# Gate bound in columns, an early convolution tile, decays two units ahead, and forget-gate sums moved forward

## The chip, the cores and the metric

The kernel runs on one core of a Trainium2 chip. The metric is device time in microseconds, the median of several runs. The five engines are TensorE (PE), VectorE (DVE), ScalarE (ACT), GpSimd (POOL) and SyncE (SP, which here issues the weight transfers). PE's weight loads are a sixth row of the profile, PEld.

## The reference

All of it is fp32, on 256 positions of width 1024. Two blocks follow each other: the first has an HGRN2 mixer, a SwiGLU, a differential attention and a mixture of eight experts; the second has a Conformer convolution, two squared-ReLU networks and a "forgetting" attention. The parts that the change touches, cut:

```python
# HGRN2: 8 heads of 128; lb_logits is (3, 1024)
q, f, i, g = split(h @ w_in, 4)
lb = cumsum(softmax(lb_logits, axis=0), axis=0)[0]
forget = lb + (1 - lb) * sigmoid(f);  log_f = log(forget);  k = 1 - forget
q = silu(q);  v = i
# per head, causal: out[t] = sum over s<=t of (q[t] * exp(sum of log_f over s+1..t)) . k[s]  v[s]
o = rms_norm(o, norm_g) * sigmoid(g);  h @ w_out follows

# Conformer convolution
u = hn @ w_pw1 + b_pw1;  a, g = split(u, 2);  u = a * sigmoid(g)
u = depthwise_causal_conv(u, w_dw, width 31) + b_dw;  layernorm, silu, @ w_pw2

# forgetting attention, 16 heads of 64
logit[t, s] = q_t.k_s / 8 + c[t] - c[s],  c = cumsum(log_sigmoid(h @ w_f + b_f))
```

## The kernel before

The program is one fixed order of instructions per engine, tied by semaphores; nothing reorders it. Its backbone is a product of fp32 matrices in three passes: every weight half of 2048 columns is split by ACT (`wh`, L762) and DVE (`wl`, L1292) into a high and a low part, the input is split in the same way (`xTh`, `xTl`), and PE adds three products (L1920 to L1922). Three `wh`/`wl` slots are used in turn. ACT and DVE each have a function `split()`, and the n-th split of DVE waits for the n-th of ACT. Each call stands by hand between other work. SP refills three weight slots of 2 MB.

A projection is a row of units (one chunk of 512 output columns, two halves of the weights, two blocks `b` of 128 positions). The results go to the two banks of `up`; the first half of the next unit waits until DVE has moved the bank of the same `b` on.

**HGRN2 projection, units 0 to 7** (0 to 126 us). The order of the chunks is `HG_CHUNKS`: 0 and 1 are q, 2 and 3 the forget gate, 4 and 5 v, 6 and 7 the output gate. The lower bound `lb` is worked out beside it: GpSimd broadcasts the three rows of logits to all 128 partitions, and DVE and ACT handle them as 128x1024 tiles (L1366 to L1380, L867). For a gate chunk DVE runs four operations per block (L1345 to L1348), ACT the sigmoid (L801) and the logarithm (L862).

**HGRN2 recurrence** (131 to 227 us). Sixteen steps m = 2*head + block. For each, PE makes the decays ("levels", L2107, four products of 512 columns into the banks `level_banks(n)`), ACT takes the exponential (L883), DVE multiplies it with q and k (L1399 to L1405, the tiles `hgA`, `hgB`), PE makes the scores into `acc[:, 2:4]` (L2123, L2126), DVE masks them into `hgS` (L1414), and PE adds up the output (L2135, L2137, "outs"). The score banks and `hgS` exist once. So the scores of m+1 wait for the mask of m, and the mask of m waits for the scores of m and for the outs of m-1 (semaphores `hg_s`, `hg_o`).

**Convolution** (1777 to 1902 us). A projection of 4 units (L1742, L1073, L1748 per block), and then 31 taps for each of 8 channel tiles. DVE does tiles 0 to 3 with 31 multiply-adds each (`tap`, L1728, L1730), a few of them between its units. PE does tiles 4 to 7 as products with diagonal matrices (L2372), which ACT writes (L1089) into a ring of 16; ACT also adds the bias (L1082). After that PE waits for both (`cv_dw`, `cv_sum`).

**Second attention** (from 2247 us). The running sums `c` of the forget gate come from small products (L2410 to L2416) placed in the q projection's second unit; ACT then copies the key side (L1142) and sends it by two DMAs (L1146) into rows of the key tiles. Queries are copied by L794, the scores are L2427.

Of the kernel before, what the change touches and what calls it, by code (L numbers as in the profile page):

```python
# [32 lines left out]
P = 128  # L33
D = 1024
# [155 lines left out]
def _program(nc, t, ctx):  # L190
# [73 lines left out]
    hg_raw = flat(arena[:, 0:2, :])[:, 0:3 * D].rearrange("p (r n) -> p r n", r=3)  # L264
    lb, omlb = spare[:, 0:D], spare[:, D:2 * D]
# [29 lines left out]
    CV_DVE, CV_PE = range(4), range(4, KT)  # L295
# [17 lines left out]
    hg_cross = tp[:, 0, 0:P]  # L313
# [17 lines left out]
    HG_CHUNKS = [0, 1, 4, 5, 2, 3, 6, 7]  # L331
# [131 lines left out]
    hg_x = sem("hg_x")  # L463
    hg_fh, hg_fl = sem("hg_fh"), sem("hg_fl")
# [28 lines left out]
    def _(sp):  # L493
# [236 lines left out]
    def _(act):  # L730
# [114 lines left out]
        split(SPLITS - 1)  # L845
        for i, c in enumerate(HG_CHUNKS):
            split()
# [15 lines left out]
            split()  # L863
            if i == 1:
                act.wait_ge(s_lbD, 1)
                for r in range(3):
                    ins = f(hg_raw[:, r, :], hg_raw[:, r, :], ACT.Exp)  # L867
                ins.then_inc(s_lbA, 1)
            elif i == 3:
# [6 lines left out]
        for x in range(2 * NB):  # L876
            at = slice((x // NB) * W, (x // NB + 1) * W)
            f(lfh[:, x % NB, at], lf[:, x % NB, at], ACT.Copy).then_inc(hg_fh, 1)
        for n in range(NH * NB + 3):
            if n < NH * NB:  # L880

                act.wait_ge(hg_m, n + 1)
                f(level_banks(n), level_banks(n), ACT.Exp).then_inc(hg_e, 1)  # L883
            if 2 <= n < NH * NB + 2:
                m = n - 2
                j, b = m // NB, m % NB
                act.wait_ge(hg_o, m + 1)
# [1630 lines left out]
```

## Time and profile before

| | |
|---|---|
| median of 3 runs | 2548.72 us (2546.42 to 2553.87) |
| the profiled execution | 2556.3 us, span 2554.5 us, mean granted clock 0.973 |
| busy: PE, PEld | 2392.2 us (94%), 1968.0 us (77%) |
| busy: DVE, ACT, POOL | 1797.1 us (70%), 1465.3 us (57%), 56.7 us (2%) |
| the chain that ended last | PE 75%, DVE 11%, ACT 7%, DMA 5%, issue 2% |

A row of a timeline gives the start in us from the span's start, the time in us that the instructions took, the engine and line, the operation with its output and inputs, how many it merges, and in brackets the idle time before it and who ended that. PE rows overlap: in a full stream one product of 512 columns starts every 0.23 us at the full clock (2.4 GHz) and every 0.43 us at half of it (1.2 GHz). The granted clock is 1.00 or 0.50 at any moment; a number between is a mean.

### The profile page before, as it was taken

The page shows a single profiled execution, that of the slowest core. Times are in us where ns is not written, and L with a number is a line of the kernel's source. Part 1 is how long each engine was busy: PE and PEld are TensorE (multiplying, and loading weights), DVE is VectorE, ACT ScalarE, POOL GpSimd, SP SyncE. Part 2 cuts the span into 40 slices and gives each one's busy share as a digit, 9 for nine tenths or more (in the row PEclk, how much of TensorE's full clock was granted, in tenths as well). Part 3 has the DMA queues.
Part 4 walks back from the last instruction along what each step waited for, and adds up shares of the span by engine and source line. Part 5 has one row for each costly group of instructions (what it writes and reads, how often), then busy time and mean ns, then how long its engine had stood idle before and what let it go on. Part 6 is the DMA issues. An engine that isn't in the chain of part 4 may idle for free.

```text
span 2554.5 us, 29769 instructions
## 1 busy us (share of the span) xinstructions
PE 2392.2 (94%) x11189; PEld 1968.0 (77%) x11189; DVE 1797.1 (70%) x1712; ACT 1465.3 (57%) x1560; POOL 56.7 (2%) x99
## 2 busy tenths in 40 slices
PE   7888999877999999999999999997989998989997
PEld 6677788666788888888888888885777887777886
DVE  5675554674889898989898988887765455554454
ACT  4532444352777777777777777775565446455344
POOL 0000000002300000000000000000010000000000
PEclk9999999998999999999999999998999999999999
DMA  8203554404999999999999999995303544413542
GB/s 296 100 4 116 182 190 167 170 34 151 330 351 370 331 385 325 382 334 378 336 378 336 379 337 369 347 369 192 140 5 132 198 181 165 151 60 132 187 161 80
DMA packets 264116, 589.69 MB, mean 231 GB/s; under 512 B 8417, under 2 KB 39377, under 8 KB 263760
## 3 DMA queue, kind: packets, MB, share of 16 engines
q1 hardware_dynamic: 261376, 579.38, 62.5%
q0 software_dynamic: 2608, 8.93, 1.0%
q8 instruction: 67, 1.10, 0.2%
q14 instruction: 33, 0.27, 0.0%
q10 hardware_dynamic: 32, 0.02, 0.0%
HBM read 587.22 MB, written 1.05 MB: 230 GB/s over the span
## 4 chain that ended last, share of the span: by engine, by line
PE 75%; DVE 11%; ACT 7%; DMA 5%; issue 2%; ACTq 0%; DVEq 0%; SPq 0%
PE up L1920 15%; PE up L1922 14%; PE up L1921 14%; PE acc L1920 7%; PE acc L1922 7%; PE acc L1921 7%; DVE wl L1292 5%; ACT wh L762 4%; DMA raw<-in_ffn_w 4%; PE up L2372 2%; PE acc L2239 1%; PE up L2137 1%; PE acc L2123 1%; PE tp L2275 1%; DVE half L1414 1%
## 5 line engine op out<-in xcount | busy, mean ns | idle before, releaser
L1609 DVE TENSOR_TENSOR wl<-raw,wh 128x2048 fp32r<-128x2048 f32 x378 | 864.7, 2291 | 127.3 <-ACT wh L980 124.6
L980 ACT ACTIVATE wh<-raw 128x2048 fp32r<-128x2048 f32 x378 | 727.1, 1924 | 227.0 <-PE up L1922 137.0
L1920 PE MATMUL up<-wh,xTh 128*128 128x512 f32 x1888 | 761.2, 403 | 46.1 <-DVE wl L1292 8.6
L1922 PE MATMUL up<-wh,xTl 128*128 128x512 f32 x1888 | 745.4, 395 | 0.0
L1921 PE MATMUL up<-wl,xTh 128*128 128x512 f32 x1888 | 744.7, 394 | 0.0
L1292 DVE TENSOR_TENSOR wl<-raw,wh 128x2048 fp32r<-128x2048 f32 x171 | 389.5, 2291 | 388.7 <-ACT wh L762 387.4
L762 ACT ACTIVATE wh<-raw 128x2048 fp32r<-128x2048 f32 x171 | 324.9, 1916 | 383.4 <-PE up L1922 212.2
L1920 PEld LDWEIGHTS up<-wh,xTh 128*128 128x128 f32 x1888 | 361.1, 191 | 129.7 <-issue 35.7
L1922 PEld LDWEIGHTS up<-wh,xTl 128*128 128x128 f32 x1888 | 360.1, 191 | 78.2
L1921 PEld LDWEIGHTS up<-wl,xTh 128*128 128x128 f32 x1888 | 361.4, 191 | 72.2 <-issue 0.7
L1920 PE MATMUL acc<-wh,hTh 128*128 128x512 f32 x848 | 330.2, 389 | 2.3 <-DVE hTl L1629 1.5
L1922 PE MATMUL acc<-wh,hTl 128*128 128x512 f32 x848 | 330.1, 389 | 0.0
L1921 PE MATMUL acc<-wl,hTh 128*128 128x512 f32 x848 | 329.9, 389 | 0.0
L1920 PEld LDWEIGHTS acc<-wh,hTh 128*128 128x128 f32 x848 | 159.2, 188 | 35.6 <-issue 2.7
L1921 PEld LDWEIGHTS acc<-wl,hTh 128*128 128x128 f32 x848 | 159.2, 188 | 33.0
L1922 PEld LDWEIGHTS acc<-wh,hTl 128*128 128x128 f32 x848 | 159.2, 188 | 33.0
L990 ACT ACTIVATE hTh<-tp 128x512 fp32r<-128x512 f32 x63 | 37.8, 600 | 76.6 <-PE tp L2275 76.6
L801 ACT ACTIVATE half<-up,sc 128x512 f32<-128x512 f32 x40 | 27.5, 689 | 55.1 <-PE up L1922 55.0
L2372 PE MATMUL up<-arena 128*128 128x256 f32 x248 | 55.8, 388 | 1.6 <-ACT arena L1089 1.6
L1321 DVE SCALAR_TENSOR_TENSOR xTl<-tp,vecs,xTh 128x128 fp32r<-128x128 f32 x112 | 30.3, 344 | 36.6 <-ACT xTh L782 36.2
L2372 PEld LDWEIGHTS up<-arena 128*128 128x128 f32 x248 | 48.2, 195 | 9.1 <-ACT arena L743 2.0
L1730 DVE SCALAR_TENSOR_TENSOR arena<-arena,wdw 128x256 f32<-128x256 f32 x120 | 51.2, 481 | 1.4
(352 smaller groups left out, 1953.0 us busy)
## 6 DMA issues: line engine op xcount, KB each, us to landing
raw<-in_moe_w_gate SPq DMA_DIRECT2D x126, 1024.0 KB, 6.4
raw<-in_moe_w_up SPq DMA_DIRECT2D x126, 1024.0 KB, 6.9
raw<-in_moe_w_down SPq DMA_DIRECT2D x126, 1024.0 KB, 5.9
raw<-in_ffn_w SPq DMA_DIRECT2D x32, 2048.0 KB, 8.9
raw<-in_hg_w_in SPq DMA_DIRECT2D x7, 2048.0 KB, 13.2
raw<-in_da_w_in SPq DMA_DIRECT2D x6, 2048.0 KB, 8.1
raw<-in_ffn_w_gate SPq DMA_DIRECT2D x11, 1024.0 KB, 6.9
raw<-in_ffn_w_up SPq DMA_DIRECT2D x11, 1024.0 KB, 11.0
```

What stands on the lines that cost most here:

```text
L762: f(wh[:, q % SPLITS, :], raw_half(q), ACT.Copy).then_inc(s_hi, 1)
L801: f(out, in_, func, **kw).then_inc(s_act, 1)
L980: f(wh[:, x % SPLITS, :], raw[:, x % RAW, :], ACT.Copy).then_inc(moe["hi"], 1)
L990: f(hTh[:, 0, :], tp[:, 0, :], ACT.Copy).then_inc(moe["Th"], 1)
L1292: V.tensor_tensor(wl[:, q % SPLITS, :], raw_half(q), wh[:, q % SPLITS, :].bitcast(F32), ALU.subtract).then_inc(s_lo, 1)
L1321: ins = V.scalar_tensor_tensor(lo[:, k, :], x[:, k, :], cols[:, gain, 4 * q + k:4 * q + k + 1], hi[:, k, :].bitcast(F32), ALU.mult, ALU.su ...
L1609: V.tensor_tensor(wl[:, x % SPLITS, :], raw[:, x % RAW, :], wh[:, x % SPLITS, :].bitcast(F32), ALU.subtract).then_inc(moe["lo"], 1)
L1730: ins = V.scalar_tensor_tensor(cT[:, k, :], src, wdw[:, k, j:j + 1], cT[:, k, :], ALU.mult, ALU.add)
L1920: mm(out, x_hi, w_hi, start=start, stop=False)
L1921: mm(out, x_hi, w_lo, start=False, stop=False)
L1922: return mm(out, x_lo, w_hi, start=False, stop=stop)
L2372: mm(up[:, k % 2, 0:SEQ], diag[:, x % DIAGS, :], uT[:, k, j:j + SEQ], start=(j == 0), stop=(j == CONV - 1)).then_inc(cv_tap, 1)
```

## The change

All edits are in the order and the form of work around the same three stages; the mixture of experts and the networks are untouched.

1. **Bound in columns.** The logits come as 24 rows of 128 (`lb_rows`), PE turns them once (`bound_turn`, in unit 0), and maximum, exponential and quotient run on 128x8 columns. DVE writes 8 diagonal blocks (`lb_diag`, one 128x1024 operation), and PE spreads them over all partitions with two products by a matrix of ones (`bound_rows`, in unit 3) into `acc[:, 2:4]`. There the gate chunks read `lb`.
2. **Order at the start.** The second block of x is loaded behind the first half of the first weight chunk. `HG_CHUNKS` becomes 0, 1, 4, 6, 2, 3, 7, 5.
3. **Recurrence.** The decays of step 0 are made inside unit 7 (`first_levels`), and those of step m+2 stand between the scores of m and the outs of m-1. The sum across blocks (`hg_cross`) moves from the scores of an odd step to the outs of an even one, and its copy from DVE to ACT. The last two splits of the projection's time move into the loop (n = 3 and 5).
4. **Convolution.** PE's tiles become 3, 5, 6, 7 and DVE's 0, 1, 2, 4. PE's first tile stands before the last transposes of the projection, the second needs only the third unit. The diagonals are made earlier, and ACT's split of the last unit stands behind 62 of them.
5. **Forget-gate sums.** `gate_totals` moves to the first q unit, `gate_rows` to the start of the second, and the key-side copy and its DMAs ahead of the query copies; the scores of the first four head pairs wait for the first two query copies only.

```diff
-    CV_DVE, CV_PE = range(4), range(4, KT)
+    CV_DVE, CV_PE = [0, 1, 2, 4], [3, 5, 6, 7]
+    EARLY_DIAGS, FIRST_DIAGS = 8, CONV + 8
...
-    HG_CHUNKS = [0, 1, 4, 5, 2, 3, 6, 7]
+    HG_CHUNKS = [0, 1, 4, 6, 2, 3, 7, 5]
...
         for i, c in enumerate(HG_CHUNKS):
-            split()
+            if i < 7:
+                split()
...
+        project(g_hg, t_hg, 8, T_x, 4, middle=lambda c: {0: bound_turn, 3: bound_rows, 7: first_levels}.get(c))
+        pe.wait_ge(s_Te, T_hgo)
+        levels(1)
+        for m in range(NH * NB + 1):
+            if m < NH * NB:
                 pe.wait_ge(hg_ab, m + 1)
                 if m >= 1:
                     pe.wait_ge(hg_sm, m)
...
+            if m + 2 < NH * NB:
+                levels(m + 2)
+            if m >= 1:
+                m -= 1
...
         for c in range(4):
             split()
...
+            if c >= 2:
+                diagonals(range(EARLY_DIAGS * (c - 2), EARLY_DIAGS * (c - 1)))
...
-            split()
+            if c < 3:
+                split()
+        diagonals(range(2 * EARLY_DIAGS, FIRST_DIAGS))
         for b in range(NB):
             step_copy(t_cv[NB * 3 + b], uT[:, :, PADC:], 3, b, 2)
...
+        diagonals(range(FIRST_DIAGS, 2 * CONV))
+        split()
+        diagonals(range(2 * CONV, CONV * len(CV_PE)))
...
-        project(g_cv, t_cv, 4, T_cv, 2, enter_cv)
-        pe.wait_ge(s_Te, T_cback)
+        project(g_cv, t_cv, 4, T_cv, 2, enter_cv, before_last=first_taps)
+        pe.wait_ge(s_Te, t_cv[5] + 1)
+        taps(1)
+        pe.wait_ge(s_Te, T_cback)
...
-                project(d["g_q"], d["t_q"], 2, d["T_q2"], 4, middle=lambda c: gate_sums if c == 1 else None)
-                pe.wait_ge(s_Te, d["T_o"])
+                project(d["g_q"], d["t_q"], 2, d["T_q2"], 4, middle=lambda c: (gate_totals, gate_rows)[c])
```

PE's order in one round of the recurrence, before: decays (`L2107`), scores (`L2121` to `L2126`), outs (`L2137`), decays.

```order
L2107 MATMUL acc<-hTh,xTh 128x512 [waits hg_scaled,hg_fl]
L2107 MATMUL acc<-hTh,xTl 128x512
L2107 MATMUL acc<-hTh,xTh 128x512
L2107 MATMUL acc<-hTh,xTl 128x512
L2121 MATMUL tp<-raw,stage 128x128 [waits hg_masked,hg_scaled]
L2123 MATMUL acc<-raw 128x128 x7
L2126 MATMUL acc<-arena 128x128
L2137 MATMUL up<-arena,half 128x128 [waits hg_gated,hg_masked]
L2137 MATMUL up<-arena,half 128x128 x7
L2107 MATMUL tp<-hTl,xTh 128x512 [waits hg_x,hg_scaled,hg_fl]
```

PE's order at the same place after the change: scores (`L2177`, `L2180`), decays (`L2155`), outs (`L2194`, `L2196`), scores.

```order
L2177 MATMUL acc<-raw 128x128 [waits hg_masked,hg_scaled]
L2177 MATMUL acc<-raw 128x128 x6
L2180 MATMUL acc<-arena 128x128
L2155 MATMUL acc<-hTh,pe_parts 128x512 [waits hg_fl]
L2155 MATMUL acc<-hTh,pe_parts 128x512 x3
L2194 MATMUL up<-arena,stage 128x128 [waits hg_x,hg_gated,hg_masked]
L2196 MATMUL up<-arena,half 128x128 x8
L2177 MATMUL acc<-raw 128x128 [waits hg_masked,hg_scaled]
```

The decays stood between the outs and the next scores, and now stand between the scores and the outs.

ACT's order at the end of the convolution's projection, before: `L762` is a split, `L743` the copy of a turned block, `L1073` the sigmoid, `L1089` a diagonal.

```order
L762 ACTIVATE wh<-raw 128x2048 [waits s_used,w_ready1]
L743 ACTIVATE arena<-tp 128x2x128 [waits s_T] x2
L1073 ACTIVATE half<-half 128x256 [waits conv_normed] x2
L762 ACTIVATE wh<-raw 128x2048 [waits s_up,w_ready2]
L743 ACTIVATE arena<-tp 128x2x128 [waits s_T] x2
L1089 ACTIVATE arena<-cst,wdw 128x128 x16
```

ACT's order at the same place after (`L767` split, `L748` copy, `L1107` sigmoid, `L1096` diagonal, `L1087` bias of a tile).

```order
L767 ACTIVATE wh<-raw 128x2048 [waits s_used,w_ready1]
L748 ACTIVATE arena<-tp 128x2x128 [waits s_T] x2
L1096 ACTIVATE arena<-cst,wdw 128x128 x8
L1107 ACTIVATE half<-half 128x256 [waits conv_normed] x2
L1096 ACTIVATE arena<-cst,wdw 128x128 [waits conv_taps] x23
L748 ACTIVATE arena<-tp 128x2x128 [waits s_T] x2
L1096 ACTIVATE arena<-cst,wdw 128x128 [waits conv_taps] x8
L1087 ACTIVATE arena<-acc,vecs 128x256 [waits conv_taps]
L1096 ACTIVATE arena<-cst,wdw 128x128
L1096 ACTIVATE arena<-cst,wdw 128x128 [waits conv_taps] x14
L767 ACTIVATE wh<-raw 128x2048 [waits s_up,w_ready2]
```

DVE's order after the change where it meets that split (`L1318` its half of a split, `L1781` and `L1787` the last block of the projection, `L1769` the multiply-adds of the convolution).

```order
L1781 SCALAR_TENSOR_TENSOR half<-up,sc,big 128x512 [waits s_up]
L1787 TENSOR_TENSOR stage<-half 128x256 [waits d_ch,s_T,s_act]
L1318 TENSOR_TENSOR wl<-raw,wh 128x2048 [waits s_hi]
L1769 SCALAR_TENSOR_TENSOR arena<-arena,wdw 128x256 [waits s_Te]
L1769 SCALAR_TENSOR_TENSOR arena<-arena,wdw 128x256
```

On ACT the split moved behind 46 diagonals that wait for PE's taps; on DVE its other half stays where it was, in front of 112 of the 124 multiply-adds.

## Rows read from the trace of the kernel before

**Rows 1.** Timeline of PE, first projection: start us, us, engine line operation, count, idle before and releaser

```profile
14.50 0.79 PE L1920 MATMUL up<-wh,xTh 128*128 128x512 f32 x1 [5.00 <-DVE wl L1292]
29.55 0.47 PE L1920 MATMUL up<-wh,xTh 128*128 128x512 f32 x1 [1.18 <-DVE stage L1352]
57.40 0.47 PE L1920 MATMUL up<-wh,xTh 128*128 128x512 f32 x1 [4.01 <-DVE arena L1354]
85.25 0.76 PE L1920 MATMUL up<-wh,xTh 128*128 128x512 f32 x1 [4.21 <-DVEq L1350]
100.76 0.47 PE L1920 MATMUL up<-wh,xTh 128*128 128x512 f32 x1 [1.93 <-DVEq L1350]
```

**Rows 2.** Windows, same stretch: stretch, length, busy us (instructions) of each engine, granted clock, DMA

```profile
50.00:60.00 10.00, 5.99 (x22) 4.56 (x22) 4.61 (x4) 8.32 (x9) 0.00 (x0) 0.89 0.19 58
60.00:70.00 10.00, 10.00 (x43) 8.15 (x42) 8.99 (x6) 2.52 (x2) 0.00 (x0) 0.94 0.40 153
```

**Rows 3.** Timelines of DVE and ACT, the same stretch

```profile
46.31 3.49 DVE L1370 TENSOR_TENSOR arena<-arena,raw 128x1024 f32<-128x1024 f32 x3
49.83 2.96 ACT L867 ACTIVATE arena<-arena 128x1024 f32<-128x1024 f32 x3 [4.46 <-DVE arena L1370]
96.19 1.28 ACT L801 ACT_TABLE_LOAD   x1 [0.71 <-PE up L1922]
```

**Rows 4.** DMA issues, 0 to 140 us: transfer, queue, count, KB each, median us to landing

```profile
arena<-in_hg_lb POOLq DMA_DIRECT2D x1, 1536.0 KB, 9.6
h<-in_x SPq DMA_DIRECT2D x2, 512.0 KB, 4.5
```

**Rows 5.** Timelines of PE and DVE, recurrence, and one row of the chain (141.63)

```profile
131.20 0.76 PE L2107 MATMUL acc<-hTh,xTh 128*128 128x512 f32 x1 [5.50 <-DVE xTl L1386]
141.63 0.46 PE tp L2121 x2
168.98 1.80 PE L2123 MATMUL acc<-raw 128*128 128x128 f32 x14 [0.48 <-DVE half L1414]
172.77 0.48 PE L2107 MATMUL acc<-hTh,xTh 128*128 128x512 f32 x1
173.12 1.23 DVE L1414 TENSOR_TENSOR half<-acc,big 128x1024 f32<-128x1024 f32 x1 [1.19 <-PE up L2137]
174.49 0.46 PE L2121 MATMUL tp<-raw,stage 128*128 128x128 f32 x2 [0.56 <-DVE half L1414]
226.34 3.60 PE L2022 MATMUL acc<-h,cst 128*128 128x512 f32 x8
```

**Rows 6.** Windows of PE, first attention: stretch, us, busy, granted clock, DMA share, GB/s

```profile
560.00:570.00 10.00, 6.50 (x42) 1.00 0.01 2
```

**Rows 7.** Timelines of PE, DVE and ACT, convolution

```profile
1828.18 0.44 PE L1954 MATMUL tp<-cst,stage 128*128 128x128 f32 x2 [2.80 <-DVE stage L1748]
1829.80 0.69 PE L1954 MATMUL tp<-cst,stage 128*128 128x128 f32 x2 [1.19 <-DVE stage L1748]
1832.07 55.80 PE L2372 MATMUL up<-arena 128*128 128x256 f32 x248 [1.58 <-ACT arena L1089]
1831.12 2.29 DVE L1292 TENSOR_TENSOR wl<-raw,wh 128x2048 fp32r<-128x2048 f32 x1 [1.38 <-ACT wh L762]
1839.71 42.51 DVE L1730 SCALAR_TENSOR_TENSOR arena<-arena,wdw 128x256 f32<-128x256 f32 x98
1831.53 8.84 ACT L1089 ACTIVATE arena<-cst,wdw 128x128 f32<-128x128 f32 x29
```

**Rows 8.** Timelines of PE and DVE, start of the second attention

```profile
2242.00 0.39 PE L2416 MATMUL acc<-cst,few_rows 128*16 128x128 f32 x2 [0.92 <-DVEq L1814]
2251.99 0.80 PE L2427 MATMUL up<-arena 128*128 128x128 f32 x2 [5.35 <-ACT raw L794]
2247.17 2.29 DVE L1292 TENSOR_TENSOR wl<-raw,wh 128x2048 fp32r<-128x2048 f32 x1 [1.25 <-ACT wh L762]
2253.25 0.61 DVE L1829 SCALAR_TENSOR_TENSOR arena<-up,few_rows,cst 128x128 f32<-128x128 f32 x2 [3.79 <-PE up L2427]
```

More of the change, by code:

```diff
@@ L857, in _ @@
                 step_act(g, half[:, g % 2, :], up[:, g % 2, :], func)
+                if i == 7 and b == 0:
+                    decays(0)
+            if i == 6:
+                act.wait_ge(s_lbA, 2)
+                f(lf_first[0], lf[:, 0, 0:W], ACT.Copy).then_inc(hg_fh, 1)
             if c in (2, 3):
@@ L862, in _ @@
                     f(lf[:, b, (c - 2) * W:(c - 1) * W], half[:, (g_hg + b) % 2, :], ACT.Ln).then_inc(s_lbA, 1)
-            split()
             if i == 1:
                 act.wait_ge(s_lbD, 1)
[L866 to L869, printed above, removed]
+                f(lb_cols[:, 0:3, :], lb_cols[:, 0:3, :], ACT.Exp).then_inc(s_lbA, 1)
+            if i < 7:
+                split()
+            if i == 3:
                 act.wait_ge(s_big, 16)
@@ L875, in _ @@
         act.wait_ge(s_lbA, 1 + 2 * NB)
-        for x in range(2 * NB):
+        act.wait_ge(s_up, g_hg + 8 * NB)
+        for x in range(1, 2 * NB):
             at = slice((x // NB) * W, (x // NB + 1) * W)
@@ L1065, in _, with conv_sum, diagonals @@
         row_roots(H_CV)
+        def conv_sum(i):
+            k = CV_PE[i]
+            act.wait_ge(cv_tap, CONV * (i + 1))
+            f(cT[:, k, :], acc[:, i, 0:SEQ], ACT.Identity, bias=rowcols[:, 0, k:k + 1]).then_inc(cv_sum, 1)
+        def diagonals(xs):
+            for x in xs:
+                if x >= DIAGS:
+                    act.wait_ge(cv_tap, x - DIAGS + 1)
+                if x % CONV == DIAGS and x > CONV:
+                    conv_sum(x // CONV - 1)
+                f(diag[:, x % DIAGS, :], ident, ACT.Copy, scale=wdw[:, CV_PE[x // CONV], x % CONV:x % CONV + 1]).then_inc(cv_diag, 1)
         for c in range(4):
@@ L1137, in _ @@
                     if c == 1:
+                        act.wait_ge(f_CT, 1)
+                        f(ncT[0:NH2, :], acc[0:NH2, 1, 0:SEQ], ACT.Copy, scale=-1.0).then_inc(f_ct, 1)
+                        act.wait_ge(f_ct, 1)
+                        act.wait_ge(s_Te, d["t_kv"][3] + 1)
+                        for z in range(2):
+                            act.dma_start(kz[z][BIAS_ROWS[z], :, :], ncT[z:NH2:2, :]).then_inc(s_kb, 16)
                         for b in range(NB):
@@ L1140, in _ @@
                     split()
-                act.wait_ge(f_CT, 1)
-                f(ncT[0:NH2, :], acc[0:NH2, 1, 0:SEQ], ACT.Copy, scale=-1.0).then_inc(f_ct, 1)
-                act.wait_ge(f_ct, 1)
-                act.wait_ge(s_Te, d["t_kv"][3] + 1)
-                for c in range(2):
-                    act.dma_start(kz[c][BIAS_ROWS[c], :, :], ncT[c:NH2:2, :]).then_inc(s_kb, 16)
                 for b in range(NB):
@@ L1360, in _ @@
                 last_turn[g % 2] = t_hg[s] if t_hg[s] is not None else last_turn[g % 2]
[L1361 to L1376 removed]
+            e3 = lb_cols
@@ L1384, in _ @@
+        for x in range(1, 2 * NB):
             at = slice((x // NB) * W, (x // NB + 1) * W)
@@ L2371, in _, with first_taps @@
                 pe.wait_ge(cv_diag, x + 1)
-                mm(up[:, k % 2, 0:SEQ], diag[:, x % DIAGS, :], uT[:, k, j:j + SEQ], start=(j == 0),
+                mm(acc[:, i, 0:SEQ], diag[:, x % DIAGS, :], uT[:, k, j:j + SEQ], start=(j == 0),
                    stop=(j == CONV - 1)).then_inc(cv_tap, 1)
+        def first_taps():
+            pe.wait_ge(s_Te, t_cv[3] + 1)
+            taps(0)
+        project(g_cv, t_cv, 4, T_cv, 2, enter_cv, before_last=first_taps)
+        pe.wait_ge(s_Te, t_cv[5] + 1)
+        taps(1)
+        pe.wait_ge(s_Te, T_cback)
+        for i in range(2, len(CV_PE)):
+            taps(i)
         pe.wait_ge(cv_dw, 1)
```

208 lines of the change are left out of this document (111 added, 97 removed).

## The prediction

> **What bounds the kernel.** I read the page first: PE is busy 94% of the span and holds 75% of the chain, so a microsecond counts where PE waits, or works more, in the stages the change touches. Then PE's timeline for its waits, and DVE's and ACT's for what ended them. In the first projection PE starts at 14.50 and waits 1.18, 4.01, 4.21 and 1.93 us later [rows 1]. The reader is to see that the big ones stand behind work on the bound: DVE 3.49 us, then ACT 2.96 us before a split [rows 3], and the same kind of work again (L1378 to L1380) before the wait of 4.21. In the recurrence PE waits only about 0.5 us per step, though DVE's mask takes 1.23 us: the decays, issued at 172.77, run beside the mask at 173.12 [rows 5]. The convolution's end is set by PE's taps, 1832.07 to 1887.87; DVE's multiply-adds end at 1882.22, 5.65 us sooner [rows 7]. The second attention starts behind a wait of 5.35 us [rows 8].
>
> All sums are made against the profiled execution, span 2554.5 us, 1.8 us around it. It lay 7.6 us above the median of 2548.72 us; the differences worked out below are put on the median.
>
> **1. Bound and projection.**
> Start: the second half of x (512 KB, landing in 4.5 us [rows 4]) no longer stands before the first weights. The first weights can't gain more than such a transfer's time nor lose by it: 0 to 4.5 us. The two transfers share the engines with what surrounds them, so I take a third, 1.6 us.
> Unit 0 to 1: the wait of 1.18 us comes from the late arrival of the second chunk. 1536 KB of broadcast logits that took 9.6 us beside it [rows 4] become 12 KB. I take it as gone: -1.2.
> Unit 2 to 3: the wait of 4.01 us goes with the wide operations, and with it the half clock that followed: mean clocks of 0.89 and 0.94 in the windows from 50 and 60 [rows 2] are 2 x (1.1 + 0.6) = 3.4 us at half rate, half of it lost: -1.7, taken as -1.6. Together -5.6.
> Unit 4 to 5: the reciprocal and its followers go. What stays is the forget-gate chain. In the wait of 1.93 us at 100.76 it is seen alone, with a table load of 1.28 us in it [rows 1, 3]. The new order puts an output-gate chunk (also a sigmoid) in front, so no load stands there: 1.93 - 1.28 = 0.65, and -3.6. PE's row at 85.25 has the half clock's form too (0.76 us, where 0.47 is the full one's); I take a little less than before: -1.2. Together -4.8.
> Unit 5 to 6 keeps its 1.93 us.
> Added: two products of ones. The residual product's 8 rows are 4 products of the same kind in 3.60 us [rows 5], so 1.8 us, and 0.2 for the turning. The decays of step 0 are in unit 7 now: four starts at 0.23, 0.9. DVE's small columns and its one diagonal operation (a 128x1024 operation, 1.23 us as the mask) stand beside PE's 11 us units, where DVE is idle for several: 0; without that cover 2.
> Sum: -1.6 - 1.2 - 5.6 - 4.8 + 2.0 + 0.9 = -10.3. From below, if new waits of DVE take half of it, -5; from above -13.
>
> The Trainium skill (ScalarE: Activation LUTs, What ACT_TABLE_LOAD costs) gives a switch of tables 1.28 us and a drain of about 1.38 on top. The row shows 1.28 and the next activation 0.02 us behind its end. By the page the load taken from the chain would give 1.4 us more, -11.7; the sum keeps to the row.
>
> **2. Seam and recurrence.** Before, the projection ends at 131.20 - 5.50 = 125.70, and the scores of step 1 start at 141.63 [rows 5], 15.9 later. Now decay and exponential of step 0 fall into unit 7. After it PE needs ACT's last activation and one copy, and one DVE difference, each of 512 columns (some 0.7 us, as half of the 1.23 of the mask's 1024 and a start): decays of step 1 run from +2.9 to +4, at half clock to +4.6; the exponential, 1.0 as one of the three in 2.96 [rows 3], to +5.5; two scalings on DVE of the mask's width to +8; mask of step 0 (1.23) to +9.2. Then the scores of step 1. Gain 15.9 - 9.2 = 6.7, between 5 and 8.
>
> In the loop I look for what waits for what. Mask m needs outs m-1, and scores m+1 need mask m: both rules stay. Before, PE went scores (168.98), outs, decays (172.77), and the mask (173.12 + 1.23) ran while PE made the decays; the next scores came at 174.49: 5.51 us. Now the decays stand between scores and outs, on the chain that leads to the mask, and nothing is left for PE to do during the mask. A round is 5.51 + the decays. Four starts of 0.23 with the first 0.31 us: 1.0. So 6.5 us and PE idle 1.5 in each. Steps 1 to 13 have decays behind them: +13.0. The cross sum moves from one side to the other of the same chain: 0. The last rounds have no decays to place, -0.4 (they waited for the copy that ACT has now).
> DVE per round: three operations of the mask's 1.23 us and a small product, so 3.9 of 6.5; each moved split (2.29 [rows 7]) just fits into the 2.6 that are free. If not, +1. ACT has one exponential, a few small ones and a split: fits.
> Sum -6.7 + 13.0 - 0.4 = +5.9 (bounds +4 and +9).
>
> **3. Convolution.** PE no longer waits 2.80 + 1.19 + 1.58 = 5.57 us: from 1828.18 - 2.80 = 1825.4 on it has 55.8 us of taps (0.45 each) and 1.2 of transposes, ready at 1882.4. But DVE's second split of the last unit follows ACT's, and that one now stands behind the 62nd diagonal, which waits for the 46th tap. 46 taps at 0.45 and 0.6 of transposes between them: 1825.4 + 21.3 = 1846.7. ACT keeps up: 29 diagonals in 8.84 us [rows 7] is 0.30 each. Its split of some 1.9 us ends at 1848.8; DVE's half, 2.29, at 1851.2. Before, DVE had it done at 1833.4. Queued behind it on DVE are 112 of 124 multiply-adds, among them the 98 that took 42.51 us. They end 17.8 us later: 1882.2 + 17.8 = 1900.0, where the taps ended at 1887.87 before and PE went on half a microsecond later. +11.7. If ACT is slower than PE here, 1.5 more. PE then has waited 19 us and turns and adds the residual at half clock: the 3.60 us become up to 7, partly beside DVE's statistics: +1.3.
> Sum +13.0 (+11 to +15).
>
> **4. Second attention.** The wait of 0.92 us goes. The last two query copies and the two DMAs leave PE's way; the scores of step 0 can come at 2251.99 - 5.35 - 0.92 = 2245.7 [rows 8]. What is late next is DVE, whose split ended at 2247.17 + 2.29 = 2249.5 and would end at 2248.5; it starts on the scores then and not at 2253.25. ACT's copies and a table load (1.28) end about then, as the first maximum comes. Sum -4.5 (-3 to -5.5).
>
> **Sum**: -10.3 + 5.9 + 13.0 - 4.5 = +4.1 us; 2548.7 + 4.1 = 2552.8, say 2553 us.
>
> **Rivals.**
> A, recurrence unharmed: if the mask doesn't bind as I read it, the loop stays at 5.5 us. +4.1 - 13.0 = -8.9: 2540 us. It is on the faster side, and decides if the scores follow the outs by less than 1.5 us. For it: nothing but the small wait of 0.5 us before; against it: the mask's releaser in every round is `PE up`. 6%.
> B, DVE not held up in the convolution: PE is ready at 1882.4 with DVE, -5.6 instead of +13: 4.1 - 18.6 = -14.5, 2534 us. Decides if DVE's long row starts before 1840. The order of the two queues speaks against it. 5%.
> C, the projection's gain stays out: the bound is no longer late, but ACT's queue (an output-gate chunk with its table load) puts a new wait of some 2 us at two unit ends, each with a half-clock stretch of 1.5. -10.3 becomes -3.3: +11, 2560 us. For it: 1.93 us from one such load at 100.76. 15%.
> D, the clock: PE's wait in each round grows from 0.5 to 1.5 us. With a fall to half clock in one round of three, 14 rounds' 4.8 us of PE work would cost some +22: 2575 us. Against it, PE at 6.50 of 10 us busy in the first attention kept 1.00 [rows 6]. The Trainium skill (TensorE: Matmul & The Clock Gate, A second HAM failure mode: psum-queue depth-cycling) tells of a kernel whose short waits between groups of products made the clock swing; by that rule D is what happens, by the row it is not. 4%.
> The forecast itself: 70%.
>
> **How the numbers follow.** What a measurement of this kernel can tell from no change is 0.3%, 7.6 us: 2541.1 to 2556.4. The forecast's own range is 2547 to 2559; about 0.58 of its 0.70 lies within 0.3%, 0.11 above. A is half below: faster gets 0.04 + 0.05 (B) + 0.02 (larger gains in the projection) = 0.11. Slower gets 0.11 + 0.13 (C) + 0.04 (D) = 0.27. The same keeps 0.62. For eight in ten the range is 2544 to 2562: it leaves out B, D and most of A.
>
> **What would show it.** Right: PE's first product at 13 and step 1's scores about 9 us behind the projection's end; 6.5 us from scores to scores, PE idle 1.5 before each with the mask as releaser; DVE's long row of multiply-adds starting near 1851 on this scale and PE waiting for it nearly 20 us; DVE's first attention row 4 us sooner. Wrong: rounds of 5.5 us, or a long DVE row before 1840, or a granted clock under 1.00 through the recurrence.

## The result and the profile after

| kernel | median | ratio to before (95%) |
|---|---|---|
| before, first comparison | 2547.54 us (5 runs, 2545.72 to 2553.87) | |
| changed | 2560.01 us (5 runs, 2559.4 to 2561.77) | 1.0042 (1.0032 to 1.0053) |
| changed, second comparison | 2561.43 us (5 runs) | 1.0039 (1.0026 to 1.0052) |

The changed kernel is slower by 0.4%, some 10 to 12.5 us, and the intervals of both comparisons lie clear of 1. The forecast was 2553 us, no measurable change, with a range of 2544 to 2562. So both medians lie in the range, by 2.0 and 0.6 us, but above the forecast's own band for no change (2541.1 to 2556.4); an outcome above that band had been given a chance of 0.27. The changed kernel's profiled execution took 2559.58 us: span 2557.8, mean granted clock 0.975, PE busy 2387.3 us (93%), DVE 1781.4 (70%), ACT 1459.7 (57%); the chain that ended last is PE 78%, DVE 11%, ACT 6%, DMA 3%, issue 2%.

PE's timeline in the first projection and the seam behind it:

```profile
11.98 1.97 PE L1940 MATMUL tp<-cst,h 128*128 128x128 f32 x8 [5.62 <-DMA h<-in_x]
14.14 0.80 PE L1959 MATMUL up<-wh,xTh 128*128 128x512 f32 x1 [0.19 <-DVE wl L1318]
76.00 0.47 PE L1959 MATMUL up<-wh,xTh 128*128 128x512 f32 x1 [1.46 <-DVEq L1401]
89.94 0.47 PE L1959 MATMUL up<-wh,xTh 128*128 128x512 f32 x1 [1.92 <-DVEq L1401]
117.02 0.76 PE L2155 MATMUL tp<-hTl,xTh 128*128 128x512 f32 x1 [2.86 <-DVE xTl L1441]
123.78 1.80 PE L2177 MATMUL acc<-raw 128*128 128x128 f32 x14 [1.35 <-DVE half L1453]
```

Set beside [rows 1, 5]: the waits of 1.18 and 4.01 us are gone, that of 4.21 is 1.46, that of 1.93 stays. The projection ends at 117.02 - 2.86 = 114.16, 11.5 us sooner, and the scores of step 1 follow 9.6 us later instead of 15.9. The first window of [rows 2], all engines, and one over the rounds of the recurrence:

```profile
50.00:60.00 10.00, 10.00 (x44) 7.96 (x43) 5.97 (x8) 5.83 (x5) 0.00 (x0) 1.00 0.58 211
120.00:212.00 92.00, 70.90 (x544) 65.91 (x543) 58.74 (x66) 24.10 (x52) 0.00 (x0) 1.00 0.00 1
```

One round of the recurrence, PE's rows and the mask of DVE:

```profile
200.98 1.80 PE L2177 MATMUL acc<-raw 128*128 128x128 f32 x14 [1.48 <-DVE half L1453]
202.76 0.48 PE L2155 MATMUL tp<-hTl,xTh 128*128 128x512 f32 x1
203.99 1.95 PE L2196 MATMUL up<-arena,half 128*128 128x128 f32 x16
207.41 1.80 PE L2177 MATMUL acc<-raw 128*128 128x128 f32 x14 [1.48 <-DVE half L1453]
199.61 1.22 DVE L1453 TENSOR_TENSOR half<-acc,big 128x1024 f32<-128x1024 f32 x1 [2.75 <-PE up L2196]
```

From scores to scores it is 6.43 us. The decays (202.76) stand ahead of the outs (203.99), and the mask waits for the outs; PE has nothing beside it.

The last outs (the 16 products behind the last mask), first in this execution and then in the third one of the changed kernel, and a window of this execution around them:

```profile
218.94 0.46 PE L2194 MATMUL up<-arena,stage 128*128 128x128 f32 x2 [1.98 <-DVE arena L1461]
219.24 3.56 PE L2196 MATMUL up<-arena,half 128*128 128x128 f32 x16
218.15 1.95 PE L2196 MATMUL up<-arena,half 128*128 128x128 f32 x16
218.00:223.00 5.00, 4.06 (x19) 3.94 (x20) 1.03 (x3) 0.17 (x1) 0.00 (x0) 0.66 0.01 2
```

PE waits 1.98 us in front of them in both. In one the clock then falls and they take 3.56 us, in the other it stays at 1.00 and they take 1.95.

The convolution, PE, DVE and ACT:

```profile
1839.55 40.33 PE L2428 MATMUL acc<-arena 128*128 128x256 f32 x186
1900.29 3.78 PE L2449 MATMUL tp<-cst,arena 128*128 128x128 f32 x16 [20.41 <-DVEq L1798]
1842.77 4.48 ACT L1096 ACTIVATE arena<-cst,wdw 128x128 f32<-128x128 f32 x15
1847.15 1.90 ACT L767 ACTIVATE wh<-raw 128x2048 fp32r<-128x2048 f32 x1
1849.09 2.29 DVE L1318 TENSOR_TENSOR wl<-raw,wh 128x2048 fp32r<-128x2048 f32 x1 [18.82 <-ACT wh L767]
1857.67 42.51 DVE L1769 SCALAR_TENSOR_TENSOR arena<-arena,wdw 128x256 f32<-128x256 f32 x98
```

The chain is: diagonals that wait for taps, then ACT's split, then DVE's split after 18.82 us of waiting, then the 98 multiply-adds, which [rows 7] had at 1839.71, and PE's 20.41 us. The windows in PE's wait and behind it (after the length comes PE's busy time; the third number from the right is the granted clock):

```profile
1880.00:1900.00 20.00, 0.00 (x0) 0.00 (x0) 19.61 (x48) 0.40 (x1) 0.00 (x0) 0.63 0.00 0
1900.00:1910.00 10.00, 8.85 (x32) 5.77 (x32) 5.17 (x13) 4.94 (x8) 0.00 (x0) 0.73 0.00 0
```

The second attention, DVE and PE. The wait of 5.35 us is gone, and DVE's split is what is late next:

```profile
2258.33 2.29 DVE L1318 TENSOR_TENSOR wl<-raw,wh 128x2048 fp32r<-128x2048 f32 x1 [1.52 <-ACT wh L767]
2260.54 0.60 DVE L1868 SCALAR_TENSOR_TENSOR arena<-up,few_rows,cst 128x128 f32<-128x128 f32 x2
2261.65 0.49 PE L2499 MATMUL up<-arena 128*128 128x128 f32 x2 [2.82 <-DVE att L1569]
```

**Stages.** One execution is not enough here, so the table gives the length of six stages in every profiled execution, cut at PE's rows: the start of the HGRN2 residual product (226.34 before), the product that ends the wait of 2.05 us in the convolution's projection (1777.72), the convolution's residual product (1890.78), the product that ends a wait of 4.55 us ahead of the second attention (2172.37), the last residual product behind the second attention (2314.75), and the span's end. A, C and E hold what the change touches; B, D and F hold nothing of it.

| execution | A | B | C | D | E | F | span |
|---|---|---|---|---|---|---|---|
| before, 1 | 226.3 | 1551.4 | 113.1 | 281.6 | 142.4 | 239.8 | 2554.5 |
| before, 2 | 226.7 | 1553.4 | 113.3 | 281.8 | 142.3 | 238.7 | 2556.2 |
| before, 3 | 227.1 | 1553.5 | 113.2 | 281.4 | 142.7 | 238.7 | 2556.6 |
| before, 4 | 224.8 | 1551.8 | 113.2 | 281.3 | 140.9 | 237.8 | 2549.8 |
| changed, 1 | 222.6 | 1555.6 | 125.7 | 281.7 | 135.7 | 236.5 | 2557.8 |
| changed, 2 | 222.7 | 1555.8 | 125.7 | 282.0 | 138.0 | 237.2 | 2561.4 |
| changed, 3 | 219.9 | 1553.4 | 125.7 | 281.9 | 139.7 | 238.6 | 2559.2 |
| bound alone | 215.7 | 1553.7 | 113.3 | 281.0 | 141.1 | 238.2 | 2543.0 |
| outs first | 211.4 | 1553.1 | 125.6 | 281.3 | 135.6 | 237.3 | 2544.5 |
| split ahead | 222.5 | 1553.3 | 107.6 | 282.7 | 135.5 | 238.5 | 2540.0 |
| both | 211.4 | 1555.3 | 107.0 | 281.3 | 139.1 | 238.9 | 2532.9 |
| convolution undone | 222.3 | 1553.3 | 113.2 | 281.1 | 137.7 | 237.6 | 2545.2 |
| second attention undone | 222.4 | 1552.4 | 125.7 | 282.0 | 141.1 | 237.6 | 2561.3 |
| order of x undone | 223.4 | 1553.5 | 125.7 | 281.6 | 135.5 | 237.1 | 2556.7 |

By means, changed less before: A -4.5, C +12.5, E -4.3, together +3.7; B, D and F +2.4, +0.4 and -1.3.

### The profile page after: what moved, and what is told of

It is laid out like the page before. It is cut to its first block, busy times and chain, and to the rows that moved or that the text cites. A ratio compares the mean times of both kernels' runs of the same rounds, so it can differ in the third digit from the quotient of the medians.

```text
span 2557.8 us, 29771 instructions
## 1 busy us (share of the span) xinstructions
PE 2387.3 (93%) x11194; PEld 1970.1 (77%) x11194; DVE 1781.4 (70%) x1703; ACT 1459.7 (57%) x1566; POOL 54.7 (2%) x99
## 4 chain that ended last, share of the span: by engine, by line
PE 78%; DVE 11%; ACT 6%; DMA 3%; issue 2%; ACTq 0%; DVEq 0%; SPq 0%
PE up L1959 15%; PE up L1961 15%; PE up L1960 15%; PE acc L1959 8%; PE acc L1961 8%; PE acc L1960 8%; DVE wl L1318 3%; ACT wh L767 3%; DMA raw<-in_ffn_w 2%; DVE arena L1769 2%; PE acc L2298 1%; PE up L2196 1%; PE tp L2334 1%; PE acc L2177 1%; PE tp L1993 1%
## 5 line engine op out<-in xcount | busy, mean ns | idle before, releaser
L1318 DVE TENSOR_TENSOR wl<-raw,wh 128x2048 fp32r<-128x2048 f32 x171 | 389.5, 2291 | 393.3 <-ACT wh L767 392.2
L767 ACT ACTIVATE wh<-raw 128x2048 fp32r<-128x2048 f32 x171 | 324.9, 1916 | 362.2 <-PE up L1961 199.1
L1940 PE MATMUL tp<-cst,h 128*128 128x128 f32 x176 | 29.3, 315 | 27.6 <-DVEq L1297 7.8
L2428 PE MATMUL acc<-arena 128*128 128x256 f32 x248 | 53.9, 379 | 0.0
L1769 DVE SCALAR_TENSOR_TENSOR arena<-arena,wdw 128x256 f32<-128x256 f32 x120 | 51.2, 481 | 1.4
```

Of the source, the lines that this page charges most:

```text
L767: f(wh[:, q % SPLITS, :], raw_half(q), ACT.Copy).then_inc(s_hi, 1)
L1318: V.tensor_tensor(wl[:, q % SPLITS, :], raw_half(q), wh[:, q % SPLITS, :].bitcast(F32), ALU.subtract).then_inc(s_lo, 1)
L1769: ins = V.scalar_tensor_tensor(cT[:, k, :], src, wdw[:, k, j:j + 1], cT[:, k, :], ALU.mult, ALU.add)
L1940: ins = nc.tensor.transpose(tp[:, tt % 2, k * P:(k + 1) * P], src[:, b, (4 * q + k) * P:(4 * q + k + 1) * P], ident)
L2428: mm(acc[:, i, 0:SEQ], diag[:, x % DIAGS, :], uT[:, k, j:j + SEQ], start=(j == 0), stop=(j == CONV - 1)).then_inc(cv_tap, 1)
```

## The experiments

All timed results are given as ratios to the kernel before on the same chip.

**Split ahead.** ScalarE's last split of the convolution's projection goes back ahead of the diagonals.

```diff
-            if c < 3:
-                split()
+            split()
         diagonals(range(2 * EARLY_DIAGS, FIRST_DIAGS))
         ...
         diagonals(range(FIRST_DIAGS, 2 * CONV))
-        split()
```

> The changed kernel with ScalarE's last split of the convolution's projection back ahead of the diagonals. Theory: that split held VectorE's split and so its 98 multiply-adds; they start before 1840 on the scale of the trace, end near 1884, and TensorE, whose taps end near 1880, waits at most 4 us: 12 to 17 us less than the changed kernel, ratio to before about 0.999. Rival: the diagonals are what binds once the split stands before them, the early taps wait for their diagonals and the gain is under 6 us. Second rival: VectorE is held by the turned tiles, not by the split, and nothing changes.

Measured: 2540.16 us, ratio 0.9949 (0.9933 to 0.9964), against 1.0039 of the changed kernel. DVE's and PE's rows:

```profile
1829.30 2.29 DVE L1316 TENSOR_TENSOR wl<-raw,wh 128x2048 fp32r<-128x2048 f32 x1 [1.37 <-ACT wh L767]
1837.89 42.51 DVE L1767 SCALAR_TENSOR_TENSOR arena<-arena,wdw 128x256 f32<-128x256 f32 x98
1837.11 40.33 PE L2426 MATMUL acc<-arena 128*128 128x256 f32 x186
1880.51 1.09 PE L2447 MATMUL tp<-cst,arena 128*128 128x128 f32 x8 [3.08 <-DVEq L1796]
```

The split's place alone held DVE. C falls from 125.7 to 107.6, 18.1 us, a little more than expected, and PE's wait from 20.41 to 3.08. The diagonals lose nothing by it: the 186 taps take 40.33 us as before. Both rivals fall.

**Outs first.** The decays of m+2 go behind the outs of m-1, still two steps ahead.

```diff
-            if m + 2 < NH * NB:
-                levels(m + 2)
+            ahead = m + 2
             if m >= 1:
                 m -= 1
                 ...
                 ins.then_inc(hg_o, 1)
+            if ahead < NH * NB:
+                levels(ahead)
```

> The changed kernel with the decays of step m+2 issued behind the outs of step m-1, and not between scores and outs; they are still two steps ahead. Theory: VectorE's mask then runs beside the decays, as before the change; a round falls from 6.43 to about 5.5 us, TensorE's wait in it from 1.48 to 0.5, and 13 rounds give 12 to 13 us; ratio to before about 0.999. Rival: VectorE or ScalarE is the bound of a round (two scalings, mask, small product and the moved splits), and the rounds stay near 6.4 us: 0 to 3 us. Second rival: the decays, now later, make the exponential and the scalings late: rounds of 6 us.

Measured: 2549.5 us, ratio 0.9991 (0.9979 to 1.0002). A round, PE and DVE:

```profile
190.96 1.80 PE L2177 MATMUL acc<-raw 128*128 128x128 f32 x14 [0.56 <-DVE half L1453]
193.04 1.95 PE L2195 MATMUL up<-arena,half 128*128 128x128 f32 x16
194.75 0.48 PE L2155 MATMUL tp<-hTl,xTh 128*128 128x512 f32 x1
196.47 1.80 PE L2177 MATMUL acc<-raw 128*128 128x128 f32 x14 [0.55 <-DVE half L1453]
195.10 1.23 DVE L1453 TENSOR_TENSOR half<-acc,big 128x1024 f32<-128x1024 f32 x1 [1.20 <-PE up L2195]
```

The mask (195.10) now runs beside the decays (194.75), and this round is 5.51 us, what one was before the change [rows 5]. PE's waits for the mask between 142 and 208 us, of the changed kernel and of this one (us in total, times, longest):

```profile
PE acc L2177 <- DVE half L1453: 16.2, 11, 1.5
```

```profile
PE acc L2177 <- DVE half L1453: 7.0, 11, 1.5
```

A is 211.4, where the changed kernel shows 222.6 in the first execution and 219.9 at the least. Of the 11.2 us against the first, 1.8 are an earlier first product (12.33 for 14.14), which the edit doesn't touch. From the scores of step 1 to the residual product it is 88.3 us for 98.8, so the edit gave 10.5 us, less than the 12 to 13 expected. The missing part stands in two rounds that stayed at 6.36 and 6.37 us, those with the two moved splits. In the first of them PE and DVE show:

```profile
128.62 1.80 PE L2177 MATMUL acc<-raw 128*128 128x128 f32 x14 [0.56 <-DVE half L1453]
131.53 1.95 PE L2195 MATMUL up<-arena,half 128*128 128x128 f32 x16
134.98 1.80 PE L2177 MATMUL acc<-raw 128*128 128x128 f32 x14 [0.57 <-DVE half L1453]
131.42 2.28 DVE L1318 TENSOR_TENSOR wl<-raw,wh 128x2048 fp32r<-128x2048 f32 x1
133.62 1.22 DVE L1453 TENSOR_TENSOR half<-acc,big 128x1024 f32<-128x1024 f32 x1
```

The outs are done at 133.48, and the mask (133.62) follows DVE's split without idle time. So in 11 of 13 rounds neither DVE's nor ACT's work was the bound, and the order of two pieces of PE's work was. In the two others the rival holds: what DVE and ACT have to do with a split among it takes some 0.85 us more than a short round has. The long rounds of the changed kernel hid this. Two steps ahead, by itself, gives nothing in the rounds: they are 5.51 us, where those before were 5.47 on average.

**Both edits.**

> The changed kernel with both edits: ScalarE's last split ahead of the diagonals, and the decays behind the outs. Theory: the two costs are independent, so the gains add: the split edit took 17 to 18 us out of the convolution in its trace, the outs edit 12 to 13 out of the recurrence; the span is about 2528 us, ratio to before 0.990 to 0.992, faster than either kernel. Rival: they share a later wait (a weight chunk or a DMA that is then late) and the sum is under 25 us, ratio 0.994 or more.

Measured: 2532.1 us, ratio 0.9922 (0.9910 to 0.9935): faster than both kernels, and 20 us below the kernel before. The stages add up, A 211.4 and C 107.0, though the span is 2532.9 us where 2528 was expected, with a ratio of 0.990 to 0.992. The two rounds with splits are 6.36 us here too. PE still waits 2.96 us behind the taps:

```profile
1871.33 1.09 PE L2448 MATMUL tp<-cst,arena 128*128 128x128 f32 x8 [2.96 <-DVEq L1796]
```

**Convolution undone.** Tiles 4 to 7 on PE after the projection and the old order of diagonals and split, all else as changed:

```diff
-    CV_DVE, CV_PE = [0, 1, 2, 4], [3, 5, 6, 7]
+    CV_DVE, CV_PE = range(4), range(4, KT)
...
-        project(g_cv, t_cv, 4, T_cv, 2, enter_cv, before_last=first_taps)
+        project(g_cv, t_cv, 4, T_cv, 2, enter_cv)
```

> The changed kernel with the convolution's part as it was before (tiles 4 to 7 on TensorE after the projection, diagonals and split in the old order), all else changed. Theory: the convolution part costs 13.1 us in the trace, so this takes 12 to 14 us from the changed kernel: about 2547 us, ratio to before about 0.999. Rival: the changed convolution costs nothing by itself and its delay only absorbs a wait that comes later anyway: 0 to 4 us.

Measured: 2544.54 us, ratio 0.9963 (0.9948 to 0.9977). C is 113.2, 12.5 us less than in the changed kernel, and the delay doesn't go into a later wait: D is the same. The timed difference to the changed kernel, 0.9963/1.0039, is some 19 us, more than the trace's 12.5. The two ratios' intervals allow about 5 us to either side; the rest is taken up below, under the sum.

**Second attention undone.**

```diff
-                project(d["g_q"], d["t_q"], 2, d["T_q2"], 4, middle=lambda c: (gate_totals, gate_rows)[c])
+                project(d["g_q"], d["t_q"], 2, d["T_q2"], 4, middle=lambda c: gate_sums if c == 1 else None)
+                pe.wait_ge(s_Te, d["T_o"])
```

> The changed kernel with the second attention's part as before: gate sums one place later, bias rows copied and sent behind the last query copies, scores held until all query tiles are turned. Theory: the part is worth 4.5 to 6 us, so the span is 2562 to 2564 us and TensorE's wait of about 5.3 us ahead of the scores of step 0 is back. Rival: VectorE's split and first score row bind anyway (it waits 2.8 us for them in the changed kernel), and the loss is under 2 us.

Measured: 2562.14 us, ratio 1.0046 (1.0032 to 1.0060), which can't be told from 1.0039 by time. In the trace the wait is back:

```profile
2262.61 0.79 PE L2495 MATMUL up<-arena 128*128 128x128 f32 x2 [5.37 <-ACT raw L799]
```

E shows the size: 142.4, 142.3, 142.7, 140.9, 141.1 and 141.1 in the six executions with the old part, mean 141.7; in the eight with the new one between 135.5 and 139.7, mean 137.1. So 4.6 us, and one pair of executions would have said anything from 1.2 to 7.2.

**Order of x undone.**

```diff
-        ld(h[:, 0, :], t["x"][0, 0:P, :], s_x[0])
+        for b in range(NB):
+            ld(h[:, b, :], t["x"][0, b * P:(b + 1) * P, :], s_x[b])
...
-                    if part == 0:
-                        ld(h[:, 1, :], t["x"][0, P:2 * P, :], s_x[1])
```

> The changed kernel with the second half of x requested ahead of the first weights, as before. In the changed kernel's trace TensorE waited 5.62 us for that half and its first product started at 14.14, against 14.50 before. Theory: the order alone is worth 0.4 to 1 us, so the first product is at 14.5 to 15 and nothing can be told by time. Rival: it was worth the 1.6 us of my forecast and something else of the change, such as the transposed bound's small transfer, gave back 1.2 us; then the product is at 13.0.

Measured: 2562.21 us, ratio 1.0047 (1.0033 to 1.0060); no difference by time. PE's start:

```profile
8.13 1.97 PE L1940 MATMUL tp<-cst,h 128*128 128x128 f32 x8 [1.68 <-DMA h<-in_x]
15.18 0.79 PE L1959 MATMUL up<-wh,xTh 128*128 128x512 f32 x1 [5.09 <-DVE wl L1318]
```

PE's first product starts at 14.50, 15.18, 14.97, 15.00, 15.18 and 15.83 in the six executions with the old order, mean 15.1, and at 14.14, 14.19, 13.26, 13.03, 12.33, 13.96, 13.04 and 13.88 with the new one, mean 13.5. So the order is worth 1.6 us by these means. This is more than I expected, and not the rival either: nothing gave the gain back; the two first executions (14.50 and 14.14) only happened to lie close together.

**Bound alone.** The kernel before with nothing but the bound in columns:

```diff
-        pool.dma_start(hg_raw, t["hg_lb"].rearrange("r n -> (r n)").partition_broadcast(P)
-                       .rearrange("p (r n) -> p r n", r=3)).then_inc(s_lb, 16)
+        pool.dma_start(lb_rows, t["hg_lb"].rearrange("r (k p) -> (r k) p", p=P)).then_inc(s_lb, 16)
...
-        project(g_hg, t_hg, 8, T_x, 4)
+        project(g_hg, t_hg, 8, T_x, 4, middle=lambda c: {0: bound_turn, 3: bound_rows}.get(c))
```

> The kernel before with one part of the change alone: the bound computed in columns, its rows made by TensorE, 12 KB of logits in place of 1536 KB. Chunk order, recurrence, convolution and second attention are as before. Theory: in the trace the waits of 1.18 and 4.01 us go with their half clock, the one of 4.21 us falls to the 1.9 that a sigmoid's table load leaves, and two products of ones (1.8 us) come in: the projection ends 6.5 to 8.5 us sooner, and the recurrence after it is untouched, so the ratio is 0.997. Rival: the new order of chunks, not the bound, took the waits away, and here they stay: under 3 us.

Measured: 2543.49 us, ratio 0.9965 (0.9953 to 0.9977). A falls from 226.3 (mean) to 215.7. The waits of 1.18 and 4.01 us are gone without the new order of chunks; the rival falls. The projection ends 11.0 us sooner (at 114.72, for 125.70), more than the 6.5 to 8.5 expected: the half clock taken away was undersized, as shown below. The wait behind the first forget-gate unit, PE, ACT and DVE, and last the sigmoid of that unit in the changed kernel:

```profile
77.39 0.47 PE L1921 MATMUL up<-wh,xTh 128*128 128x512 f32 x1 [1.45 <-DVEq L1351]
70.61 1.92 ACT L765 ACTIVATE wh<-raw 128x2048 fp32r<-128x2048 f32 x1 [1.20 <-PE up L1923]
72.54 1.28 ACT L804 ACT_TABLE_LOAD   x1
73.83 0.60 ACT L804 ACTIVATE half<-up 128x512 f32<-128x512 f32 x1
72.56 2.29 DVE L1293 TENSOR_TENSOR wl<-raw,wh 128x2048 fp32r<-128x2048 f32 x1 [1.58 <-ACT wh L765]
71.86 0.60 ACT L806 ACTIVATE half<-up 128x512 f32<-128x512 f32 x1 [0.74 <-PE up L1961]
```

Here the old order of chunks leaves the table load in front of the sigmoid, and the wait is 1.45 us; the changed kernel has no load there and waits 1.46. DVE's split runs to 74.85, longer than load and sigmoid together (74.43): in this unit the load was not on the chain.

**The unchanged kernels again**, each profiled anew.

> The kernel before, unchanged, run and profiled once more. The changed kernel's profiled span lies 3.3 us over that of before, its median 12.5 us. Theory: the profiled execution of before carried about 9 us by chance, in stages that the change doesn't touch (its stretches 227 to 640 us and 2334 to 2500 us); this profile then has a span of about 2546 us, and the offsets between it and the changed kernel stay level in those two stretches. Rival: the recorded execution is typical and the changed kernel loses 9 us where no record shows it; then the span is 2554 again and the timed runs lie apart from it. Timed against itself: 1.000.

> The changed kernel, unchanged, timed and profiled once more beside the kernel before. In the first comparison the medians lay 12.5 us apart (five runs each), the two profiled spans 3.3 us. Twelve runs of before have since spread from 2547.8 to 2558.1 us with granted clocks from 0.973 to 0.976. Theory: the distance lies between, since runs of both kernels differ by half-clock stretches that come and go: ratio 1.002 to 1.004, and the steps of the trace repeat (first product near 14, scores of step 1 near 124, rounds of 6.43, a wait near 20 us behind the taps). Rival: the five runs of before were typical and the ratio is 1.005 or more.

> The kernel before, one more profiled execution. Its two profiled executions so far took 2556.3 and 2558.1 us, while the median of its timed ones is 2551. Theory: executions differ by stretches of half clock behind the same waits, so an execution near 2548 shows some stages shorter by 1 to 2 us each at the same waits. Rival: one stage alone is shorter by 6 us or more.

> The kernel before, a fourth profiled execution, with the same two theories as the third: many stages shorter by 1 to 2 us each at the same waits, or one stage shorter by 6 us or more.

> The changed kernel, a third profiled execution beside the kernel before's third and fourth on the same chip. Theory: its convolution takes 125.7 us again, its first part 222.6, its second attention between 106 and 109, and only the clock's stretches differ. Rival: one of the stages that the change doesn't touch is longer than in every execution of before by 3 us or more, which would be a cost of the change that I have not priced.

Measured: before 0.9999 (0.9988 to 1.0010) against itself, in 12 runs from 2547.84 to 2558.05 us; the changed kernel 1.0039. The profiled executions of before took 2558.05, 2558.46 and 2551.67 us, the third of the changed kernel 2561.02. Before's third and fourth differ by 6.8 us in the span, and by the table by 2.3 (A), 1.7 (B), 1.8 (E) and 0.9 (F): many stages, no single one. The same stretch in both (in the third it starts 4.12 us later, as its stage E does), with PE busy as long and the clock 0.94 in the third, 1.00 in the fourth, which got more instructions done (162 for 154):

```profile
2274.12:2304.12 30.00, 27.84 (x154) 22.18 (x153) 12.98 (x37) 13.32 (x39) 1.28 (x2) 0.94 0.09 27
```

```profile
2270.00:2300.00 30.00, 27.84 (x162) 22.67 (x160) 14.04 (x37) 13.24 (x38) 1.28 (x2) 1.00 0.09 27
```

That supports the theory of half-clock stretches that come and go. The changed kernel's third execution has A at 219.9 where 222.6 was expected, C at 125.7 as expected, and no untouched stage 3 us longer than in every execution of before. The theory doesn't reach as far as I expected: before 2, expected at 2546, had a span of 2556.2, and the low runs of before (2546 us) were never caught in a profile.

## Why the prediction was right, and where it was not

The number fell inside the range. The mechanisms were right for the most part and the total of the trace was too, but part of that is luck, as errors of the terms cancelled; and the call of no measurable change was not right. The terms in turn:

**Projection** (forecast -10.3; trace -11.5). The bound was what PE waited for, as said: alone it takes 10.6 us out of A. Within the sum, the start is right by means (-1.6 forecast, -1.6) but only -0.4 in the executions compared here. The waits gave 8.0 us for the 8.8 forecast, and what was added is, as the rest, some 2.1 us for 2.9. Unit 4 to 5 has the wrong reason: I took the table load off the wait of 1.93 us and expected 0.65, and 1.46 is left, with the load or without. The 1.93 that I read [rows 1, 3] belongs to the second gate unit, where ACT's sigmoid ends DVE's wait; in the first, DVE's split ends later. DVE's first row behind that wait in the second gate unit of the changed kernel:

```profile
87.31 0.69 DVE L1396 TENSOR_TENSOR half<-half,raw 128x512 f32<-128x512 f32 x1 [1.27 <-ACT half L806]
```

The new order of chunks gives nothing at the first. Where the Trainium skill (ScalarE: Activation LUTs, What ACT_TABLE_LOAD costs) counts a drain of some 1.4 us beside the load, these rows show the load 0.01 us behind the split before it (70.61 + 1.92) and the next activation 0.01 us behind the load (72.54 + 1.28, then 73.83). What made up for it is half clock that went behind the starts of the units: the same product stands 10.5 us sooner at 87.94 of before and 11.8 sooner at 104.37, with the wait between them unchanged. The whole projection, before and then changed:

```profile
14.00:126.00 112.00, 99.74 (x416) 80.24 (x416) 70.83 (x58) 59.95 (x57) 0.00 (x0) 0.95 0.51 187
14.00:114.00 100.00, 96.35 (x425) 77.99 (x425) 56.80 (x58) 59.68 (x57) 2.25 (x3) 1.00 0.55 198
```

Before, 33 of its products start 0.43 us apart, in the changed kernel 7. At 0.20 us each that is 5.2 us, and the sum had 1.6 and 1.2 for it. It is the most undersized term of this part.

**Seam** (-6.7; trace -6.3) and **rounds** (6.5 us with PE idle 1.5; trace 6.43 with 1.48). Right in place, releaser and size; outs first shows the cause, 10.5 us of 13 rounds' 12, with two rounds held by the splits. The split moved into a round was priced as just fitting the long round, and it did. The end was not right: -0.4 was forecast for the last rounds, and behind the wait of 1.98 us the last outs ran at half clock in the first two executions (3.56 us for 1.95), which the sum had not. So from the scores of step 1 to the residual product it is 14.1 us more than before in these two, and 12.5 in the third, where 12.6 had been forecast. The net of the HGRN2 stages, -10.3 + 5.9 = -4.4, is -4.5 by the means of A. In the first execution it is -11.5 - 6.3 + 14.1 = -3.7: the projection's excess and the last outs' loss cancel, and that is luck.

**Convolution** (+13.0; C is +12.5 by means, with the half clock behind the wait in it). DVE's long row started at 1857.67, behind a split that ended at 1851.4 (1851.2 forecast), and PE went on at 1900.29 (1900.0). The 1.3 us for the half clock are there: from PE's first turn to the residual product it is 3.57 us (1900.29 to 1903.86), and 2.30 before.

**Second attention** (-4.5; -4.6 by means in the experiment above). DVE's split is late next, as said: it ends at 2260.6, and PE's and DVE's rows just ahead of it lie 11 us later than before, so at 2249.6 on the old scale, against 2248.5 forecast.

**Rivals.** A (rounds unharmed) and B (DVE not held) did not happen, and are what the two edits bring about: each took out about its price (10.5 of 13.0, and 18.1 of 18.6). C: a wait near 1.9 us at two unit ends is there (1.46 and 1.92), but it was there before, and the gain came in. D did not happen: PE waited 1.48 us in each round and the granted clock was 1.00 over all of 120 to 212 us; it fell only behind them, for the last outs. The Trainium skill (TensorE: Matmul & The Clock Gate, A second HAM failure mode: psum-queue depth-cycling), taken for this kernel as the prediction took it, would have made it swing; this trace doesn't agree for such rounds.

**The sum.** The forecast was +4.1 us. The touched stages say +3.7, the profiled spans +5.2 by means (2554.3 and 2559.5), the timed medians +10.9 and +12.5. So the terms add up to what the traces show, and the forecast is 7 to 8 us below the medians. The range held with little to spare, and no term of it stood for this error. Rival C's 2560 us is the measured number, but not by C's way. The step that failed is the first one: that the differences worked out on a profiled execution may be put on the median. The four profiled executions of before took 2556.1 us on average, its four medians 2550.7; the three of the changed kernel lie within 2 us of its medians.

Why the low runs of before are not matched by low runs of the changed kernel (10 timed, none under 2559.4, while 35 runs of before on one chip spread over 13 us) stays open. No stage that the change leaves alone is longer by more than 2.4 us. One pattern is on record. Take each kernel's profiled span less the mean of before's (2554.3), and beside it the timed difference by its ratio. In the four kernels without the convolution's long wait (bound alone, split ahead, both, convolution undone) the timed difference lies from 0.4 below to 2.3 us above the trace's. In the four with it (changed, outs first, second attention undone, order of x undone) it lies 4.7 to 9.6 above. That points at the long wait, or at what follows it. But outs first had low runs too (2544.9 to 2556.0 us), all but the changed kernel have one profile each, and no run was made to test it.

## What to carry to other kernels

Before work is moved ahead in an engine's queue, ask what else that engine did while it waited: the decays cost nothing as long as they ran beside the mask, and a full microsecond per round once they stood before what releases it. Where the n-th split of one engine waits for the n-th of another, a split moved behind something that is paced by a third engine's progress moves everything queued behind its partner too. An engine that isn't the bound in a long round can become it once the round is short: the two moved splits cost nothing at 6.43 us and some 0.85 us each at 5.51. And a sum made on one profiled execution can agree with the traces and be 7 us off the median, so profile the kernel before more than once where the answer hangs on 0.3%.

## What the runs showed of the hardware

- The same kernel on the same chip took 2546 to 2559 us, and its mean granted clock went with it (35 runs): spans, by means, of 2554 us at 0.973, 2551 at 0.974, 2547 at 0.975, 2546 at 0.976. By these means a thousandth of the clock was some 2.4 us.
- The granted clock stayed 1.00 through rounds of 6.43 us with PE waiting 1.48 us in each (PE busy 70.90 of 92 us), and fell in a wait of 20.41 us (mean 0.63), with 0.73 in the 10 us after it. Behind a single wait of 1.98 us it fell in two executions (mean 0.66 from 218 to 223 us) and stayed 1.00 in a third.
- A table load of 1.28 us was free where the consumer was still busy with its own queue: PE waited 1.45 us with it and 1.46 without. It followed the split before it by 0.01 us, and the next activation followed it by 0.01 us.
